# Attention stages of a decoder trunk: TensorE runs a unit's projection steps ahead of its scores

## Chip, cores and metric

The kernel runs on one core of a Trainium2 chip. The metric is the device time of one execution in microseconds (us). Every kernel was run several times; a time below is a median.

## What is computed

Two post-norm layers over 512 tokens of width 1024 in float32. Layer 0 mixes tokens with native sparse attention (16 heads of 64; a compressed branch, a selected branch and a window branch; for 512 tokens the last two see every earlier token). Layer 1 mixes with "forgetting" attention (a softmax with a cumulative gate bias). Each mixer is followed by a gated MLP with a causal convolution of width 3. Cut to what matters:

```
for i in range(2):
    y = nsa_mixer(x, ...) if i % 2 == 0 else fox_mixer(x, ...)
    x = layer_norm(ALPHA * x + y, ln1_g[i], ln1_b[i])
    x = layer_norm(ALPHA * x + conv_ffn(x, ...), ln2_g[i], ln2_b[i])

# nsa, per head:  q,k rotated;  softmax(q k / 8, causal) v  for ks,vs and for kw,vw,
#                 plus softmax(q k_cmp) v_cmp over 31 compressed blocks, three learned gates
# fox, per head:  softmax(q k / 8 + cum_q - cum_k, causal) v
```

## The kernel before

Every engine has its own instruction list, written out by hand, and the lists meet only at named semaphores. Activations lie transposed (width on the 128 partitions, 512 tokens along the row). A float32 operand is split into a high and a low part of type float32r, and each product is three matmuls: high x high, low x high, high x low (`mm3`, lines 908 to 911).

**A unit** is one attention block: a head's 128 queries against their keys, for one branch. In layer 0 (128 units) a head has eight: four query blocks i = 0 to 3, each for the selected and for the window branch; w = 0 to 7 is the unit's place in its head and i = w // 2. In layer 1 (64 units) a pair of heads has eight, v = 0 to 7, with i = v % 4. A unit goes through TensorE three times, with other engines in between:

- S, the scores (`nsa_scores`, `fox_scores`; lines 1067 and 1281, the bias 1282, the causal mask 1052);
- VectorE takes the row maximum (line 1425), ScalarE the exponential (line 625), VectorE the reciprocal of the sum (1433) and the scaling (1436 in layer 0, 1439 in layer 1);
- T, the transpositions of the probabilities (`turn`, line 1098, i + 1 of them);
- ScalarE copies the high part (line 640), VectorE takes the low part (`unit_lo`, line 1451, semaphore `pt_lo`);
- P, the value products (`pv`, 3(i + 1) small matmuls on lines 909 to 911; in every second unit of layer 0 a compressed product on line 1120 goes ahead of them).

In the loop step of unit u, TensorE runs S of u+2, then K, then P of u-2, then T of u. K is one of the projection steps (`kstep`, line 937) of later heads: three matmuls of 512 columns. Layer 0 has one K in each of the first 96 units, eight to a projected item. Layer 1 has four in v = 0 to 3 and two in v = 4 to 7 of pairs 0 to 6 (pair 0 lacks those of v = 0 and 1). At w = 0 and v = 0 T stands ahead of K.

The other engines keep the same beat: in the step of u, VectorE does max of u+2, scale of u+1 and low part of u-1; ScalarE does exp of u+2 and high part of u. Extra work is put at fixed places: in layer 0 ScalarE copies a finished item at w = 7, between exp of u+2 and the high part (`item_copy`, lines 595 and 597); VectorE computes the compressed branch's softmax from w = 4 on (`cmp_difference`, line 1473, at w = 5). In layer 1 ScalarE copies the projected values at v = 7 after exp of u+2 (`fox_value_copy`, line 847), and VectorE takes their low part at v = 1 after its max and scale (`fox_lo`, line 1714).

Three waits guard the projections' PSUM banks. K of w = 0 waits for the copy of the item before (`proj_copied`). The first K at v = 0 waits for the value copy (`proj_copied`), and the first K at v = 2 for the values' low part (`proj_lo`). GpSimd takes the low part of each weight block (line 433) once ScalarE has taken the high part (line 526), in layer 0 at w = 4.

Of the kernel before, what the change touches and what calls it, by code (L numbers as in the profile page):

```python
# [34 lines left out]
GROUPS, REP = 4, 4  # L35
# [15 lines left out]
R = 3  # L51
# [27 lines left out]
def build_trunk(nc, t, out):  # L79
    with ExitStack() as ctx:  # L80
# [3 lines left out]
        def sem(name):  # L84
            return ctx.enter_context(nc.semaphore(name))
# [130 lines left out]
        s_pf = sem("proj_copied")  # L216
# [690 lines left out]
        def _(pe):  # L907
            def mm3(o, ah, al, bh, bl, start, stop):
                nc.tensor.matmul(o, ah, bh, start=start, stop=False)  # L909
                nc.tensor.matmul(o, ah, bl, start=False, stop=False)  # L910
                return nc.tensor.matmul(o, al, bh, start=False, stop=stop)  # L911
# [25 lines left out]
            def kstep(c, slot, k, bank=BP):  # L937
                if k == 0:
                    pe.wait_ge(s_wl, c + 1)
                last = mm3(ps[:, bank, :], wh[:, slot, k, :], wl[:, slot, k, :], xh[:, k, :], xl[:, k, :], k == 0, k == KB - 1)  # L940
                if k == KB - 1:
                    last.then_inc(s_wu, 1)
# [108 lines left out]
            def mask(bank, i, stop=True):  # L1051
                return nc.tensor.matmul(ps[:, bank, i * P:(i + 1) * P], identb[:, :], causalb[:, :], start=False, stop=stop)  # L1052

            def nsa_scores(u):
                g, v = u // 32, u % 32
                h, i, br = v // 8, v % 8 // 2, v % 2
                par = g % 2
                if v % 8 == 0:

                    pe.wait_ge(s_pl, 4 * g + 3 + h // 2)  # L1060
                    if h == 0:
                        pe.wait_ge(s_sw[par], 32 * (g // 2 + 1))
                if u >= 2:
                    pe.wait_ge(s_ex, u - 1)
                n, b = (i + 1) * P, BS + u % 2
                for part in range(2):
                    nc.tensor.matmul(ps[:, b, 0:n], qs[par][:, h, i * P:n], (ks, kw)[br][par][:, part, 0:n], start=part == 0, stop=False)  # L1067
                mask(b, i).then_inc(s_sc, 1)

            def cmp_scores(H):  # L1070
                g, h = H // 4, H % 4
                rows = slice(h % 2 * HD, h % 2 * HD + HD)

                n = min(H + 3, NSA_ITEMS) - 1
                if n % 4 == 1:
                    pe.wait_ge(s_pl, n + 1)
                else:
                    pe.wait_ge(s_r2, n - (n + 2) // 4 + 1)

                pe.wait_ge(s_pf, 4 * g + 3 + h // 2)  # L1080
                for i in range(QT):
                    last = nc.tensor.matmul(ps[:, BX, i * NCMP:(i + 1) * NCMP], qf[g % 2][rows, h // 2, i * P:(i + 1) * P],
                                            kcd[rows, g * NCMP:(g + 1) * NCMP], start=True, stop=True)
                last.then_inc(s_cs, 1)

            def cmp_turn(H):

                pe.wait_ge(s_cp, H + 1)
                for i in range(QT):
                    last = nc.tensor.transpose(ps[0:NCMP, BX, i * P:(i + 1) * P], csm[:, i, :], ident[:, :])  # L1090
                last.then_inc(s_ct, 1)

            def turn(u, loc):
                pe.wait_ge(s_pr, u + 1)
                if not isinstance(u, int) or u >= 2:
                    pe.wait_ge(s_ptl, u - 1)
                for kt in range(loc[1] + 1):
                    last = nc.tensor.transpose(ps[:, BT + loc[0] % 2, kt * P:(kt + 1) * P], prob[:, loc[0] % 4, kt * P:(kt + 1) * P], ident[:, :])  # L1098
                last.then_inc(s_pt, 1)
# [10 lines left out]
            def nsa_pv(u):  # L1110
                g, v = u // 32, u % 32
                h, i, br = v // 8, v % 8 // 2, v % 2
                H = 4 * g + h
                bank = BO + H % 2
                if v % 8 == 0:
                    if H >= 2:
                        pe.wait_ge(s_ol, H - 1)
                    pe.wait_ge(s_cc, H + 1)
                if br == 0:
                    nc.tensor.matmul(ps[0:HD, bank, i * P:(i + 1) * P], vcd[:, g, :], pct[0:NCMP, H % 2, i * P:(i + 1) * P], start=True, stop=False)  # L1120
                cs = slice(br * HD, (br + 1) * HD)
                pv(u, (u, i), bank, vh[g % 2][:, :, cs], vl[g % 2][:, :, cs], False, br == 1)
# [10 lines left out]
            for g in range(GROUPS):  # L1133
                for v in range(32):
                    u = 32 * g + v
                    if u + 2 < NSA_UNITS:
                        nsa_scores(u + 2)
                    if v % 8 == 0:

                        turn(u, (u, v % 8 // 2))  # L1140
                    if g < GROUPS - 1:
                        n = 4 * (g + 1) + v // 8
                        if v % 8 == 0:
                            pe.wait_ge(s_pf, n)
                        kstep(4 + n, (4 + n) % R, v % 8)
                    if v % 8 == 4 and u + 4 < NSA_UNITS:
                        cmp_scores(u // 8 + 1)
                    if u >= 2:
                        nsa_pv(u - 2)
                    if v % 8 == 0:  # L1150
                        cmp_turn(u // 8)
                    else:
                        turn(u, (u, v % 8 // 2))
                    if v % 8 == 1 and (g < GROUPS - 1 or v == 1):

                        pe.wait_ge(s_cc, u // 8 + 1)
                        item_turn(*((g + 1, v // 8 - 1) if v > 1 else (g, 3)))
# [112 lines left out]
            def fox_scores(u, v, par, pair, rows_landed):  # L1270

                h, i = v // 4, v % 4
                if v == 0:
                    pe.wait_ge(s_pl, NSA_ITEMS + 3 * pair + 2)
                    pe.wait_ge(s_bl[par], rows_landed)
                if v == 4:
                    pe.wait_ge(s_plb, pair + 1)
                pe.wait_ge(s_ex, u - 1)
                n, b = (i + 1) * P, BS + v % 2
                for part in range(2):  # L1280
                    nc.tensor.matmul(ps[:, b, 0:n], fqs[par][:, h, i * P:n], fkd[par][:, h, part, 0:n], start=part == 0, stop=False)  # L1281
                nc.tensor.matmul(ps[:, b, 0:n], biasq[par][0:4, h, i * P:n], biask[par][0:4, h, 0:n], start=False, stop=False)  # L1282
                mask(b, i).then_inc(s_sc, 1)
# [11 lines left out]
            def fox_stages(pair, par, rows_next, first=False, more=True):  # L1295
                U = NSA_UNITS + 8 * pair
                for v in range(8):
                    if v + 2 < 8:
                        fox_scores(U + v + 2, v + 2, par, pair, None)
                    elif more:  # L1300
                        fox_scores(U + v + 2, v - 6, 1 - par, pair + 1, rows_next)
                    if v == 0:
                        turn(U + v, (v, v % 4))
                    if more:

                        for s in range(*FOX_STEPS[v]):
                            if first and s < KB:
                                continue
                            r, k = s // KB, s % KB
                            if k == 0 and r:  # L1310

                                pe.wait_ge(s_pl, NSA_ITEMS + 3 * (pair + 1) + r - 1)
                            if k == 0 and not r:

                                pe.wait_ge(s_pf, NSA_ITEMS + pair + 1)
                            kstep(C_FOX + 3 * (pair + 1) + r, (C_FOX + r) % R, k, (BP, BX, BP)[r])
                    if v >= 2:
                        fox_pv(U + v - 2, v - 2, par, pair)
                    elif not first:
                        fox_pv(U + v - 2, v + 6, 1 - par, pair - 1)  # L1320
                    if v:
                        turn(U + v, (v, v % 4))
                    if v == 0 and not first:

                        pe.wait_ge(s_plb, pair + 1)
                        value_turn(NSA_ITEMS + pair + 1)
# [9 lines left out]
            with pe.Fori(0, 3) as i:  # L1336
                for r in range(2):

                    fox_stages(1 + r + 2 * i, (1 + r) % 2, 32 * (2 + i))
# [489 lines left out]
```

## Time and profile before

| | |
|---|---|
| median of 3 runs | 1564.2 us (1561.87 to 1565.9) |
| span of the profiled execution | 1563.1 us |
| TensorE busy in it | 1489.1 us (95%) |
| VectorE, ScalarE, GpSimd busy | 860.3, 700.9, 598.0 us |
| layer 0, units with K | about 93 to 353 us of the span |
| layer 1, pairs 1 to 6 | about 917 to 1097 us, 30 us a pair |

The profile comes from one execution, so sums are made on its span of 1563.1 us; the median of the runs lies 1.1 us above it. A busy TensorE is not TensorE at its peak, since matmuls overlap: time is read from start to start. Line numbers are those of the kernel.

### The profile page before, as it was taken

Reading aid. Unit: us, or ns where it says so; the run is one execution under the profiler, and the core shown is the slowest. Engines: PE = TensorE matmul, PEld = TensorE weight load, DVE = VectorE, ACT = ScalarE, POOL = GpSimd, SP = SyncE. Lnnn points to the kernel's source line nnn. Section 1 sums busy time; section 2 is a strip of 40 time slices with the busy share of each in tenths; the row PEclk is TensorE's granted clock in tenths of the full one; section 3 lists DMA queues with packets and bytes.
Section 4 is the critical chain, followed back from the end, with each engine's and each line's share of the span. In section 5 each row is a group of like instructions: output and inputs, shape, how many; then the busy total and the mean of one; then the engine's idle time right before and its main releaser. Section 6 shows DMA issues by size and latency. Waiting matters only on the chain.

```text
span 1563.1 us, 22861 instructions
## 1 busy us (share of the span) xinstructions
PE 1489.1 (95%) x8010; PEld 1171.6 (75%) x8010; DVE 860.3 (55%) x1549; ACT 700.9 (45%) x1292; POOL 598.0 (38%) x294
## 2 busy tenths in 40 slices
PE   8989999998998999999998999999989999999997
PEld 6867676777756888888885677777757888888884
DVE  3268877787786434342136667777886433431134
ACT  3445555558434444443133555555334444442132
POOL 2442323220245444444446422222255444444441
PEclk9999999999999999999999899999999999999999
DMA  9321111100121333333332112111221333333321
GB/s 268 76 57 42 23 33 29 41 28 2 50 73 41 108 94 94 95 94 105 102 89 70 45 46 65 54 41 55 67 68 54 94 105 94 96 94 98 97 75 54
DMA packets 219065, 113.80 MB, mean 73 GB/s; under 512 B 23136, under 2 KB 216596, under 8 KB 218996
## 3 DMA queue, kind: packets, MB, share of 16 engines
q1 hardware_dynamic: 218356, 110.80, 24.9%
q10 hardware_dynamic: 640, 2.10, 0.5%
q8 instruction: 42, 0.69, 0.2%
q14 instruction: 27, 0.22, 0.0%
HBM read 108.55 MB, written 2.23 MB: 71 GB/s over the span
## 4 chain that ended last, share of the span: by engine, by line
PE 80%; DVE 12%; issue 3%; ACT 3%; POOL 1%; DMA 1%; SPq 0%; DVEq 0%; POOLq 0%; ACTq 0%
PE ps L909 22%; PE ps L911 21%; PE ps L910 21%; PE ps L1098 3%; PE ps L1067 2%; DVE cstat L1473 2%; PE ps L1282 1%; DVE z L1630 1%; PE ps L1281 1%; DVE negmax L1425 1%; DVE z L1608 1%; PE ps L1052 1%; PE ps L1162 1%; DVE z L1621 1%; PE ps L990 1%
## 5 line engine op out<-in xcount | busy, mean ns | idle before, releaser
L433 POOL TENSOR_TENSOR wl<-raw,wh 128x1024 fp32r<-128x1024 f32 (+1 forms) x196 | 468.5, 2391 | 782.2 <-ACT wh L526 782.0
L909 PE MATMUL ps<-xh,wh 128*128 128x512 f32 x1008 | 408.6, 405 | 2.0 <-POOL wl L433 2.0
L911 PE MATMUL ps<-xh,wl 128*128 128x512 f32 x1008 | 394.7, 392 | 0.0
L910 PE MATMUL ps<-xl,wh 128*128 128x512 f32 x1008 | 394.1, 391 | 0.0
L526 ACT ACTIVATE wh<-raw 128x1024 fp32r<-128x1024 f32 (+1 forms) x196 | 202.7, 1034 | 230.2 <-PE ps L911 212.1
L911 PEld LDWEIGHTS ps<-xh,wl 128*128 128x128 f32 x1008 | 190.0, 189 | 40.4
L909 PEld LDWEIGHTS ps<-xh,wh 128*128 128x128 f32 x1008 | 191.8, 190 | 37.7 <-issue 1.8
L910 PEld LDWEIGHTS ps<-xl,wh 128*128 128x128 f32 x1008 | 190.7, 189 | 34.3 <-issue 0.2
L1653 DVE SCALAR_TENSOR_TENSOR work<-ps,conv,work 128x511 f32<-128x511 f32 x88 | 66.0, 750 | 221.6 <-ACT work L772 157.6
L1425 DVE TENSOR_REDUCE negmax<-ps 128x1 f32<-128x128 f32 (+1 forms) x192 | 93.6, 488 | 108.4 <-PE ps L1052 105.9
L625 ACT ACTIVATE prob<-ps,negmax 128x128 f32<-128x128 f32 (+1 forms) x192 | 101.2, 527 | 102.4 <-DVE negmax L1425 100.5
L909 PE MATMUL ps<-gh,wh 128*128 128x512 f32 x352 | 138.6, 394 | 0.0
L911 PE MATMUL ps<-gh,wl 128*128 128x512 f32 x352 | 137.0, 389 | 0.0
L910 PE MATMUL ps<-gl,wh 128*128 128x512 f32 x352 | 137.0, 389 | 0.0
L640 ACT ACTIVATE pth<-ps 128x128 fp32r<-128x128 f32 (+1 forms) x192 | 83.5, 435 | 113.5 <-PE ps L1098 84.9
L1451 DVE TENSOR_TENSOR ptl<-ps,pth 128x128 fp32r<-128x128 f32 (+1 forms) x192 | 92.8, 483 | 3.7 <-ACT pth L640 3.0
L1098 PE MATMUL ps<-ident,prob 128*128 128x128 f32 x480 | 90.2, 287 | 2.5 <-DVE ptl L1451 1.7
L909 PE MATMUL ps<-pth,vh 128*64 128x128 f32 x320 | 68.4, 238 | 23.7 <-DVE ptl L1451 23.6
L775 ACT ACTIVATE gh<-work 128x512 f32 (+1 forms) x44 | 27.8, 632 | 119.0 <-DVE work L1665 119.0
L1678 DVE SCALAR_TENSOR_TENSOR z<-z,ps 128x512 f32<-128x512 f32 x10 | 6.9, 688 | 129.5 <-PE ps L911 129.5
L909 PEld LDWEIGHTS ps<-gh,wh 128*128 128x128 f32 x352 | 66.1, 188 | 14.6 <-issue 1.0
L910 PEld LDWEIGHTS ps<-gl,wh 128*128 128x128 f32 x352 | 66.1, 188 | 14.6 <-issue 1.0
(211 smaller groups left out, 2519.9 us busy)
## 6 DMA issues: line engine op xcount, KB each, us to landing
raw<-in_ffn_w_up SPq DMA_DIRECT2D x88, 512.0 KB, 3.8
raw<-in_ffn_w_down SPq DMA_DIRECT2D x32, 512.0 KB, 4.1
raw<-in_fox_w_in SPq DMA_DIRECT2D x24, 512.0 KB, 3.8
raw<-in_nsa_w_in SPq DMA_DIRECT2D x12, 512.0 KB, 5.0
raw<-in_ffn_w_down SPq DMA_DIRECT2D x16, 384.0 KB, 3.5
raw<-in_nsa_w_in SPq DMA_DIRECT2D x16, 256.0 KB, 3.7
raw<-in_nsa_w_o SPq DMA_DIRECT2D x8, 512.0 KB, 4.0
raw<-in_fox_w_o SPq DMA_DIRECT2D x8, 512.0 KB, 4.2
```

Of the source, the lines that this page charges most:

```text
L433: nc.gpsimd.tensor_tensor(wl[:, slot, 0:nk, :], raw[:, slot, 0:nk, :], wh[:, slot, 0:nk, :].bitcast(F32), ALU.subtract).then_inc(s_wl, 1)
L526: nc.scalar.activation(wh[:, slot, 0:nk, :], raw[:, slot, 0:nk, :], ACT.Copy).then_inc(s_wh, 1)
L625: nc.scalar.activation(prob[:, loc[0] % 4, 0:n], ps[:, BS + loc[0] % 2, 0:n], ACT.Exp, bias=negmax[:, loc[0] % 4:loc[0] % 4 + 1], accum_ou ...
L640: nc.scalar.activation(pth[:, loc[0] % 2, 0:n], ps[:, BT + loc[0] % 2, 0:n], ACT.Copy).then_inc(s_pth, 1)
L909: nc.tensor.matmul(o, ah, bh, start=start, stop=False)
L910: nc.tensor.matmul(o, ah, bl, start=False, stop=False)
L911: return nc.tensor.matmul(o, al, bh, start=False, stop=stop)
L1067: nc.tensor.matmul(ps[:, b, 0:n], qs[par][:, h, i * P:n], (ks, kw)[br][par][:, part, 0:n], start=part == 0, stop=False)
L1098: last = nc.tensor.transpose(ps[:, BT + loc[0] % 2, kt * P:(kt + 1) * P], prob[:, loc[0] % 4, kt * P:(kt + 1) * P], ident[:, :])
L1425: nc.vector.tensor_reduce(negmax[:, loc[0] % 4:loc[0] % 4 + 1], ps[:, BS + loc[0] % 2, 0:n], AX.X, ALU.max, negate=True).then_inc(s_nm, 1)
L1451: nc.vector.tensor_tensor(ptl[:, b, 0:n], ps[:, BT + b, 0:n], pth[:, b, 0:n].bitcast(F32), ALU.subtract).then_inc(s_ptl, 1)
L1653: nc.vector.scalar_tensor_tensor(out=buf[:, 1:SEQ], in0=ps[:, bank, 0:SEQ - 1], scalar=conv[:, l, 1, bass.ds(blk, 1)], in1=buf[:, 1:SEQ], ...
```

## The change

In the loops of both layers the K steps of a unit are moved to the front of the unit, ahead of S (and, at w = 0 and v = 0, ahead of T). The waits that K carries move with it. Nothing is added or removed, and no other engine's list is touched.

```
             for g in range(GROUPS):
                 for v in range(32):
                     u = 32 * g + v
-                    if u + 2 < NSA_UNITS:
-                        nsa_scores(u + 2)
-                    if v % 8 == 0:
-
-                        turn(u, (u, v % 8 // 2))
                     if g < GROUPS - 1:
                         n = 4 * (g + 1) + v // 8
                         if v % 8 == 0:
                             pe.wait_ge(s_pf, n)
                         kstep(4 + n, (4 + n) % R, v % 8)
+                    if u + 2 < NSA_UNITS:
+                        nsa_scores(u + 2)
+                    if v % 8 == 0:
+
+                        turn(u, (u, v % 8 // 2))
...
             def fox_stages(pair, par, rows_next, first=False, more=True):
                 U = NSA_UNITS + 8 * pair
                 for v in range(8):
+                    if more:
+
+                        for s in range(*FOX_STEPS[v]):
...
+                            if k == 0 and r:
+
+                                pe.wait_ge(s_pl, NSA_ITEMS + 3 * (pair + 1) + r - 1)
+                            if k == 0 and not r:
+
+                                pe.wait_ge(s_pf, NSA_ITEMS + pair + 1)
+                            kstep(C_FOX + 3 * (pair + 1) + r, (C_FOX + r) % R, k, (BP, BX, BP)[r])
                     if v + 2 < 8:
                         fox_scores(U + v + 2, v + 2, par, pair, None)
```

TensorE's list at the turn from w = 7 to w = 0 in layer 0. `ident,prob` is T, `ks,qs` is S, `xh,wh` begins K. Before:

```order
L1098 MATMUL ps<-ident,prob 128x128 x3
L1067 MATMUL ps<-ks,qs 128x256 [waits exps]
L1067 MATMUL ps<-ks,qs 128x256
L1052 MATMUL ps<-causalb,identb 128x128
L1098 MATMUL ps<-ident,prob 128x128 [waits pt_lo,probs]
L909 MATMUL ps<-xh,wh 128x512 [waits w_lo,proj_copied]
L910 MATMUL ps<-xl,wh 128x512
L911 MATMUL ps<-xh,wl 128x512
```

And now:

```order
L1098 MATMUL ps<-ident,prob 128x128 x3
L909 MATMUL ps<-xh,wh 128x512 [waits w_lo,proj_copied]
L910 MATMUL ps<-xl,wh 128x512
L911 MATMUL ps<-xh,wl 128x512
L1067 MATMUL ps<-ks,qs 128x256 [waits exps]
L1067 MATMUL ps<-ks,qs 128x256
L1052 MATMUL ps<-causalb,identb 128x128
L1098 MATMUL ps<-ident,prob 128x128 [waits pt_lo,probs]
```

K and its wait for the copied item now follow the last T of w = 7 directly.

TensorE's list in layer 1 from v = 7 to v = 0 (`fkd,fqs` and `biask,biasq` are S). Before:

```order
L1098 MATMUL ps<-ident,prob 128x128 x3
L1278 ISA
L1281 MATMUL ps<-fkd,fqs 128x384 [waits exps]
L1281 MATMUL ps<-fkd,fqs 128x384
L1282 MATMUL ps<-biask,biasq 128x384
L1052 MATMUL ps<-causalb,identb 128x128
L1096 REGISTER_ALU [waits probs]
L1098 MATMUL ps<-ident,prob 128x128 [waits pt_lo]
L1315 REGISTER_ALU
L939 ISA [waits proj_copied]
L909 MATMUL ps<-xh,wh 128x512 [waits w_lo]
```

And now:

```order
L1098 MATMUL ps<-ident,prob 128x128 x3
L1309 REGISTER_ALU
L939 ISA [waits proj_copied]
L909 MATMUL ps<-xh,wh 128x512 [waits w_lo]
L910 MATMUL ps<-xl,wh 128x512
```

S of v = 2 and T of v = 0 no longer stand between the last T of v = 7 and the wait for the value copy.

TensorE's list in layer 1 from v = 1 to v = 2. Before:

```order
L1098 MATMUL ps<-ident,prob 128x128
L1278 REGISTER_ALU [waits odd_keys_lo]
L1281 MATMUL ps<-fkd,fqs 128x128 [waits exps]
L1281 MATMUL ps<-fkd,fqs 128x128
L1282 MATMUL ps<-biask,biasq 128x128
L1052 MATMUL ps<-causalb,identb 128x128
L1312 REGISTER_ALU
L939 REGISTER_ALU [waits proj_lo]
L909 MATMUL ps<-xh,wh 128x512 [waits w_lo]
```

And now:

```order
L1098 MATMUL ps<-ident,prob 128x128
L1306 REGISTER_ALU
L939 REGISTER_ALU [waits proj_lo]
L909 MATMUL ps<-xh,wh 128x512 [waits w_lo]
L910 MATMUL ps<-xl,wh 128x512
```

The wait for the values' low part now stands ahead of S of v = 4 instead of behind it.

## Rows read from the trace of the kernel before

**Rows 1.** The profile page: its span.

```profile
span 1563.1 us, 22861 instructions
```

**Rows 2.** The list of waits, TensorE: total us, times, longest.

```profile
PE ps L909 <- DVE ptl L1451: 25.8, 23, 1.7
...
PE ps L1067 <- ACT prob L625: 2.5, 1, 2.5
```

**Rows 3.** Busy time by stretch: stretch, length, engines busy, clock, DMA; layer 1.

```profile
977.00:1007.00 30.00, 30.00 (x191) 23.61 (x190) 21.57 (x41) 16.73 (x38) 7.19 (x3) 1.00 0.19 53
```

**Rows 4.** Timeline, TensorE, layer 0, w = 6, 7: start, duration, instruction, wait.

```profile
190.41 0.42 PE L1067 MATMUL ps<-ks,qs 128*128 128x128 f32 x2
...
190.70 0.48 PE L909 MATMUL ps<-xh,wh 128*128 128x512 f32 x1
...
193.68 0.28 PE L909 MATMUL ps<-pth,vh 128*64 128x128 f32 x1 [1.67 <-DVE ptl L1451]
...
195.35 0.63 PE L910 MATMUL ps<-xl,wh 128*128 128x512 f32 x1
```

**Rows 5.** Timeline, VectorE, layer 0, the step of w = 5.

```profile
190.04 0.55 DVE L1436 TENSOR_SCALAR prob<-prob,rinv,gate 128x512 f32<-128x512 f32 x1
190.50 2.33 DVE L1473 TENSOR_SCALAR cstat<-cstat 128x4 f32<-128x4 f32 x1
```

**Rows 6.** The instructions of line 1473: count, shortest, median, longest in ns.

```profile
L1473 DVE TENSOR_SCALAR cstat<-cstat x16: 161/2331/2334, 84.6 to 387.8; 128x4 f32<-128x4 f32 x16
```

**Rows 7.** Timeline, GpSimd: one weight block in layer 0, one in layer 1.

```profile
190.29 2.51 POOL L433 TENSOR_TENSOR wl<-raw,wh 128x1024 fp32r<-128x1024 f32 x1 [0.87 <-ACT wh L526]
...
1008.99 2.40 POOL L433 TENSOR_TENSOR wl<-raw,wh 128x1024 fp32r<-128x1024 f32 x1 [6.55 <-ACT wh L526]
```

**Rows 8.** Timeline, TensorE: S behind K; P behind the mask.

```profile
89.42 0.33 PE L1067 MATMUL ps<-ks,qs 128*128 128x128 f32 x2
...
89.63 0.41 PE L1067 MATMUL ps<-kw,qs 128*128 128x128 f32 x2
...
379.95 0.25 PE L909 MATMUL ps<-pth,vh 128*64 128x128 f32 x1
380.04 0.23 PE L910 MATMUL ps<-ptl,vh 128*64 128x128 f32 x1
```

**Rows 9.** Timeline, TensorE, layer 0, w = 7: K, P, T, then S of the next unit.

```profile
173.98 0.47 PE L909 MATMUL ps<-xh,wh 128*128 128x512 f32 x1
...
174.76 0.23 PE L909 MATMUL ps<-pth,vh 128*64 128x128 f32 x1
...
175.30 0.62 PE L1098 MATMUL ps<-ident,prob 128*128 128x128 f32 x4
175.68 0.48 PE L1067 MATMUL ps<-ks,qs 128*128 128x256 f32 x2
```

**Rows 10.** Timeline, ScalarE, layer 0, w = 7: exp, then the item's copy.

```profile
174.59 0.37 ACT L625 ACTIVATE prob<-ps,negmax 128x128 f32<-128x128 f32 x1
...
174.96 0.60 ACT L597 ACTIVATE qf<-ps 128x512 f32<-128x512 f32 x1
```

**Rows 11.** Timeline, TensorE, layer 1, v = 1: the mask that ends S.

```profile
1008.08 0.23 PE L1052 MATMUL ps<-causalb,identb 128*128 128x128 bf16 x1
```

**Rows 12.** Timeline, ScalarE, layer 1, v = 7: exp, then the value copy.

```profile
1001.72 0.47 ACT L625 ACTIVATE prob<-ps,negmax 128x256 f32<-128x256 f32 x1 [0.90 <-DVE negmax L1425]
...
1002.19 0.59 ACT L847 ACTIVATE work<-ps 128x512 f32<-128x512 f32 x1
```

**Rows 13.** Timeline, VectorE, layer 1: max of v = 7; then the step of v = 1.

```profile
1001.28 0.41 DVE L1425 TENSOR_REDUCE negmax<-ps 128x1 f32<-128x256 f32 x1
...
1008.35 0.69 DVE L1425 TENSOR_REDUCE negmax<-ps 128x1 f32<-128x512 f32 x1 [3.54 <-PE ps L1052]
...
1009.14 2.46 DVE L1439 TENSOR_SCALAR prob<-prob,rinv 128x384 f32<-128x384 f32 x1
1011.52 0.68 DVE L1714 TENSOR_TENSOR fvl<-ps,fvh 128x512 fp32r<-128x512 f32 x1
```

More of the change, by code:

```diff
@@ L1297, in fox_stages @@
                 for v in range(8):
[L1298 to L1303, printed above, removed]
                     if more:
@@ L1316, in fox_stages @@
                             kstep(C_FOX + 3 * (pair + 1) + r, (C_FOX + r) % R, k, (BP, BX, BP)[r])
+                    if v + 2 < 8:
+                        fox_scores(U + v + 2, v + 2, par, pair, None)
+                    elif more:
+                        fox_scores(U + v + 2, v - 6, 1 - par, pair + 1, rows_next)
+                    if v == 0:
+                        turn(U + v, (v, v % 4))
                     if v >= 2:
```

## The prediction

> **What bounds the kernel now.** I read the list of waits first, then the stretches, then the timelines of one head and one pair. The span is 1563.1 us [rows 1] and TensorE is the engine that everything ends on. In the loops that the change touches it hardly waits. In layer 1 it is busy for all 30.00 us of a pair [rows 3]: the pairs last as long as TensorE's list. In layer 0 the list of waits holds 23 waits for `pt_lo`, 25.8 us in all [rows 2]; 12 of them are one and the same, 1.67 us ahead of P at w = 6 of each of the 12 heads with K [rows 4]. Behind it stands VectorE's line 1473, a four-column instruction that takes 2.33 us there and 0.161 us at its shortest [rows 5, 6]. It starts at 190.50, while GpSimd's weight block runs from 190.29 to 192.80, and it ends at 192.83 [rows 5, 7]. So a VectorE instruction of this kind that starts inside GpSimd's is held to its end.
>
> So TensorE has nothing to gain from doing the same work in another order, except at that wait and in the gaps between instructions. What must be asked is whether the other engines still deliver in time. Before, K stood between S and P: while K ran, the others had time for max, exp and scale of the scores just made. Now K stands between T and S. All that hangs on S starts one K later (0.78 us from 173.98 to 174.76 [rows 9], two to four times nearly as much in layer 1), and it still has to be done by the same P, T and K.
>
> **Gaps between instructions.** S behind K takes 0.21 us to the next S (89.42 to 89.63 [rows 8]); S behind T takes 0.29 us to K (190.41 to 190.70 [rows 4]), for the same 128 columns. That gives 0.08 us a unit. P behind the mask starts its second matmul after 0.09 us [rows 8], where nine matmuls of a P behind K take 0.54 us, 0.06 each (174.76 to 175.30 [rows 9]); that takes 0.03 back. K follows T instead of the mask; I cost that at nothing. So -0.05 us in each of 96 units of layer 0 and 54 of layer 1: **-7.5 us**. Each side rests on one or two rows; the ends are 0 and -12 (150 x 0.08).
> The Trainium skill (TensorE: Matmul & The Clock Gate, Back-to-back issue gap) has the gap follow from the columns of a matmul and its weight load, with nothing for a change of kind. By it this term would be zero and the sum 28 instead of 21. The two S above differ at equal columns, so I go by the rows.
>
> **The first unit.** At the first unit of layer 0 TensorE waits 2.5 us at S for an exponential [rows 2]; one K now runs inside that wait: **-0.8 us**.
>
> **P at w = 6, layer 0.** In the step of w = 5 VectorE does max of w = 7 (it waits for S), scale, line 1473, one more, the low part that P waits for. Scale starts now at 190.04, just ahead of GpSimd's start at 190.29 [rows 5, 7]. With S a K later, scale would start at about 190.75, inside GpSimd's instruction, whose own start hangs on T and ScalarE and does not move. A scale that starts inside one is held too: in layer 1 one started at 1009.14, just after GpSimd's 1008.99, and ended at 1011.60, 0.2 us after GpSimd's end at 1011.39 [rows 7, 13]. So scale ends near 193.0, line 1473 follows with 0.2 us, and from its end to P are 0.85 us (192.83 to 193.68 [rows 4, 5]): P at 194.05 instead of 193.68. Twelve heads at 0.37: **+4.5 us**. Bounds: 0 if scale still slips in, 0.7 (a whole K) if nothing of the delay is absorbed, 0 to +8.4.
>
> **K at w = 0, layer 0: a new wait.** K waits for the item copy, which ScalarE does at w = 7 behind exp of u+2, which waits for max, which waits for S; S now stands behind K at w = 7. From the mask of that S to the start of max are 0.27 us (1008.08 to 1008.35 [rows 11, 13]), from max to exp of 128 columns about 0.32 (an estimate: 0.44 for 256 columns, 1001.28 to 1001.72 [rows 12, 13], less 0.12 for half the columns), from exp to the copy 0.37 (174.59 to 174.96), the copy 0.60 [rows 10], and 0.05 to TensorE: 1.61. TensorE needs from that mask to the end of T 0.04 + 0.57 for P (0.54 + 0.03) + 0.38 for T (175.30 to 175.68 [rows 9]): 0.99. The wait is 0.62, before it was none, since S and T lay between. It comes in 11 heads (the first item is copied before the loop): **+6.8 us**. Bounds 0.3 and 0.9 a head, +3.3 to +10.
>
> **First K at v = 0, layer 1: a new wait.** The same with 256 columns: 0.27, 0.44, 0.47 to the copy (1001.72 to 1002.19), 0.59 for it [rows 12], 0.05: 1.82 after the mask. TensorE needs 0.04 + 0.39 for six matmuls of P + 0.38 for T: 0.81. The wait is at least 1.0. Max cannot start at once, though: in the kernel before it already started the moment VectorE was free, at 1001.28 [rows 13], and now VectorE's own work ahead of it, low parts that hang on S and K of v = 5 and 6, comes some 0.6 later while the mask falls at about 1001.1 (counted through from v = 4 in the same way). I take 1.4 us; six pairs (1 to 6): **+8.4 us**, bounds 0.8 and 1.7, +5 to +10.
>
> **First K at v = 2, layer 1: a new wait.** It waits for the values' low part, which VectorE does after max and scale of the step. From the mask: 0.27 to max, 0.79 to scale (1008.35 to 1009.14), 0.4 for an unheld scale (0.46 for 512 columns, 190.04 to 190.50 [rows 5]), 0.65 for the low part (0.68 [rows 13]), 0.05: 2.15. TensorE needs 0.04 + 0.75 for twelve matmuls + 0.17 for T: 0.96. Wait 1.15, six pairs: **+6.9 us**, bounds 0.9 and 1.4, +5.4 to +8.4. Before, four K lay behind the mask and covered it.
>
> **Small waits.** By the same counting P at w = 3, v = 5 and v = 7 find their low part within 0.2 us of the moment that they want it. I put 0.1 a head and 0.2 a pair, **+2.4 us**, 0 to 5. All other waits (S for its bank, T for the scaled probabilities, K at v = 4) keep over 1 us in this counting. S a K later loosens its own wait, which costs nothing now.
>
> **Sum.** -7.5 - 0.8 + 4.5 + 6.8 + 8.4 + 6.9 + 2.4 = +20.7 us on 1563.1, and with the 1.1 us between span and median 1564.2 + 20.7 = 1584.9, so **1585 us**, 1.3% slower. The term ends, added, give +1 to +41; they will not all fall to one side.
>
> **Rivals.**
>
> Faster: the new waits stay hidden. The point is whether the item and value copies end before the last T (0.99 and 0.81 us after the mask). That needs ScalarE and VectorE to be 0.6 to 1.4 us quicker than the rows, for instance if max could start on a part of S. Then the gaps and the first unit are left: -8.3, 1556 us. Against it: five links, each with its row, and in order on each engine.
>
> No change: the wait at w = 6 breaks up. If GpSimd's weight block started 1.3 us later in relation to VectorE (its ScalarE half slipping behind), scale and line 1473 would run ahead of it, and some 1.4 of the 1.67 us would go: 12 x 1.4 = 16.8, and the +4.5 with it, 20.7 - 21.3, about 1564 us. Against it: ScalarE takes that half from T of w = 4, ahead of the exp that comes late.
>
> Slower still: the clock. After the wait at 193.68 the second matmul of a K takes 0.63 us, longer than the 0.48 of the slower first one at 190.70 [rows 4]: the lower of the two levels, 1.2 GHz. Of the 12 equal waits in layer 0 two were followed by such a stretch; my estimate is 1.5 us lost in each (some 3 us of work at half speed). In layer 1, with no waits, the granted clock is 1.00 [rows 3]. Now layer 1 has 12 waits of over 1 us and layer 0 11 more. At two in twelve that is three or four more stretches, +5; at every second one +18: 1590 to 1603 us.
> [...]
>
> Partly: one of the four larger terms is absent: 1570 to 1578 us.
>
> That the change does nothing is excluded by TensorE's list.
>
> **Chances.** Forecast as worked out (1577 to 1591) 0.62; clock beyond that 0.12; partly 0.10; no change 0.08; faster 0.08. A measurement of this kernel can tell about 0.3% from no change, 4.7 us. Slower takes the first three less 0.01, 0.83; same 0.09; faster 0.08. The range takes in the forecast, most of partly and the first part of the clock case: 1569 to 1597.
>
> **What the profile will show.** The list of waits should name for line 909 ScalarE's copies (lines 595/597: 11 waits of 0.6; line 847: 6 of 1.4) and VectorE's line 1714 (6 of 1.1), and the waits for `pt_lo` at w = 6 should be near 2.1 us, with line 1436 or 1439 held by GpSimd instead of line 1473. A pair of layer 1 should last 32.3 instead of 30.0 us. I am wrong if these waits are absent, if the pairs keep 30 us, or if half-clock stretches outweigh the waits.

## The result

| | median of the runs | |
|---|---|---|
| before | 1564.6 us (1561.9 to 1565.9, 4 runs) | |
| after | 1594.0 us (1591.5 to 1599.1, 4 runs) | ratio 1.0199, 95% interval 1.0179 to 1.022 |

The changed kernel is 29.4 us slower: 1.9% by the medians, 2.0% by the ratio in the table. The forecast was 1585 us with a range of 1569 to 1597: the direction and the new waits were right, and the centre was 9 us low. The profiled execution of after took 1599.1 us with a span of 1597.3, 5 us above its median, so sums from traces are made on the spans: 1563.1 to 1597.3, +34.2 us. What sets this execution apart from the other three is the clock (see the sum below).

The page of after and its list of waits, TensorE (total us, times, longest), beside [rows 1, 2]:

```profile
span 1597.3 us, 22861 instructions
```

```profile
PE ps L909 <- DVE ptl L1451: 29.7, 30, 2.0
...
PE ps L909 <- ACT work L847: 6.4, 6, 1.1
PE ps L909 <- DVE fvl L1714: 6.1, 6, 1.0
...
PE ps L1067 <- ACT prob L625: 1.4, 1, 1.4
PE ps L909 <- ACT work L595: 1.3, 4, 0.4
...
PE ps L909 <- ACT qf L597: 0.7, 2, 0.4
```

Three entries are new, the three guards of the projections' banks: ScalarE's item copies (595, 597), its value copy (847), VectorE's low part of the values (1714). The first entry grew and the first unit's wait (1067) shrank. A recorded wait ahead of K begins at the modelled end of T, 0.24 us after the moment at which K could have started by start-to-start times: 1.06 recorded is 1.30 of delay.

**Layer 0, w = 6.** Timelines of VectorE, GpSimd and TensorE in after (start, duration, instruction, wait); they answer to [rows 4, 5, 7]:

```profile
173.18 2.37 POOL L433 TENSOR_TENSOR wl<-raw,wh 128x1024 fp32r<-128x1024 f32 x1 [0.19 <-ACT wh L526]
...
173.62 2.21 DVE L1436 TENSOR_SCALAR prob<-prob,rinv,gate 128x512 f32<-128x512 f32 x1
174.18 0.33 PE L1067 MATMUL ps<-ks,qs 128*128 128x128 f32 x2
174.36 0.23 PE L1052 MATMUL ps<-causalb,identb 128*128 128x128 bf16 x1
...
175.75 0.16 DVE L1473 TENSOR_SCALAR cstat<-cstat 128x4 f32<-128x4 f32 x1
...
176.14 0.55 DVE L1451 TENSOR_TENSOR ptl<-ps,pth 128x384 fp32r<-128x384 f32 x1
...
176.75 0.27 PE L909 MATMUL ps<-pth,vh 128*64 128x128 f32 x1 [1.80 <-DVE ptl L1451]
```

GpSimd's weight block starts at 173.18. The scaling, due just ahead of it before, starts 0.44 us behind its start and is held to its end (2.21 us where [rows 5] has 0.55). Line 1473 behind it takes 0.16 us instead of 2.33. So the hold changed its victim, and P waits 1.77 to 2.04 us instead of 1.67.

**A pair of layer 1.** Busy time by stretch, after: one whole pair from first K to first K (columns as in [rows 3]), and its three waits from the timeline of TensorE:

```profile
1062.16:1094.84 32.68, 30.36 (x188) 23.73 (x189) 16.97 (x41) 16.01 (x38) 7.15 (x3) 1.00 0.17 49
```

```profile
1062.16 0.49 PE L909 MATMUL ps<-xh,wh 128*128 128x512 f32 x1 [1.06 <-ACT work L847]
...
1072.92 0.49 PE L909 MATMUL ps<-xh,wh 128*128 128x512 f32 x1 [1.02 <-DVE fvl L1714]
...
1092.74 0.27 PE L909 MATMUL ps<-pth,fvh 128*64 128x128 f32 x1 [0.23 <-DVE ptl L1451]
```

A pair took 30.0 us without a pause in TensorE's busy time; now it takes 32.68 with 30.36 busy. The third wait, ahead of P at v = 7, is new as well.

**The clock.** Three stretches in layer 0 and two pairs in layer 1 show what the rest of the loss is made of; first after around the wait at 176.75, then a whole pair with a half-clock stretch and one without, in the kernel of experiment 2, which has the same layer 1:

```profile
174.00:177.00 3.00, 1.20 (x11) 0.84 (x10) 2.93 (x7) 0.78 (x4) 1.55 (x1) 1.00 0.07 14
177.00:180.00 3.00, 3.00 (x25) 2.72 (x23) 1.74 (x7) 1.23 (x5) 0.00 (x0) 0.66 0.76 161
180.00:183.00 3.00, 3.00 (x21) 2.53 (x20) 2.86 (x7) 1.54 (x5) 1.28 (x1) 0.77 0.00 0
```

```profile
978.32:1012.58 34.26, 31.94 (x189) 24.85 (x189) 16.97 (x41) 16.00 (x38) 7.14 (x3) 0.95 0.17 46
912.96:945.64 32.68, 30.36 (x188) 23.71 (x189) 16.97 (x41) 16.00 (x38) 7.14 (x3) 1.00 0.18 50
```

Behind the wait the granted clock falls to the lower level, 1.2 GHz, for some 3 us: 3 x 0.34 + 3 x 0.23 = 1.7 us of clock. The pair in which this happens takes 34.26 instead of 32.68, 1.58 us more. I added up 3 us x (1 - clock) over all stretches of 3 us with a clock below 0.97, up to the end of each trace's span: 21.8 us in before, 33.8 in after. In the heads with K and pairs 1 to 6 there are 2 such stretches before and 12 after (8 and 4).

**The sum on the spans.** A head of layer 0 without such a stretch takes mostly 20.96 us before and 21.64 after (20.54 and 21.36 where the item is values): 0.71 a head on the mean of eleven, +7.8. Six pairs at 2.68: +16.1. First unit: -1.1. Clock: +12.0. Together +34.8, measured +34.2.

The agreement is closer than the parts are. From its first T to that of the first unit without K, layer 0 takes 14.0 us more, where its waits (6.7) and six more half-clock stretches (10.2) add up to 16.9: in five heads such a stretch lies where the wait ahead of K at w = 0 would be, and no wait is recorded there. Pairs 0 to 6 of layer 1 take 22.1 us more. The rest of the span is 1.9 us shorter: before happens to have three stretches more there.

The clock also explains why the profiled execution of after is the slowest. Its mean granted clock is 0.979, that of the other three 0.982 to 0.983: they lose 27 to 29 us by (1 - clock) x span, some 5 to 7 us less than the profiled one. By this estimate the median has 22.8 us of waits and gaps and some 7 of clock, against 29.4 measured.

### The profile page after: what moved, and what is told of

The parts are those of the page before. It is cut to its first block, busy times and chain, and to the rows that moved or that the text cites. A ratio compares the mean times of both kernels' runs of the same rounds, so it can differ in the third digit from the quotient of the medians.

```text
span 1597.3 us, 22861 instructions
## 1 busy us (share of the span) xinstructions
PE 1503.6 (94%) x8010; PEld 1191.7 (75%) x8010; DVE 835.9 (52%) x1549; ACT 693.2 (43%) x1292; POOL 595.0 (37%) x294
## 4 chain that ended last, share of the span: by engine, by line
PE 78%; DVE 13%; issue 3%; ACT 3%; POOL 1%; DMA 0%; DVEq 0%; SPq 0%; ACTq 0%; POOLq 0%
PE ps L909 22%; PE ps L910 21%; PE ps L911 21%; PE ps L1098 2%; PE ps L1067 2%; DVE negmax L1425 2%; DVE prob L1436 2%; DVE z L1630 1%; PE ps L1282 1%; PE ps L1281 1%; DVE z L1608 1%; PE ps L1052 1%; PE ps L1162 1%; DVE ptl L1451 1%; PE ps L1120 1%
## 5 line engine op out<-in xcount | busy, mean ns | idle before, releaser
L909 PE MATMUL ps<-xh,wh 128*128 128x512 f32 x1008 | 416.2, 413 | 16.7 <-ACT work L847 6.4
L910 PE MATMUL ps<-xl,wh 128*128 128x512 f32 x1008 | 398.1, 395 | 0.0
L909 PEld LDWEIGHTS ps<-xh,wh 128*128 128x128 f32 x1008 | 192.9, 191 | 59.7 <-issue 19.2
L911 PEld LDWEIGHTS ps<-gh,wl 128*128 128x128 f32 x352 | 66.1, 188 | 13.7
```

## Experiments

The runs of the kernel before are those made beside each set. "S first" at some w or v means that there the scores stand ahead of K, as in the kernel before. w and v name the loop step; the S in it belongs to the unit two steps later. Diffs are against the changed kernel unless said.

### 1 and 2. One layer at a time

In experiment 1 the block of `fox_stages` is put back as it was (first diff) and layer 0 stays changed; in experiment 2 the loop of layer 0 is put back (second diff) and layer 1 stays changed.

```
                 for v in range(8):
+                    if v + 2 < 8:
+                        fox_scores(U + v + 2, v + 2, par, pair, None)
...
                     if more:
```

```
                     u = 32 * g + v
+                    if u + 2 < NSA_UNITS:
+                        nsa_scores(u + 2)
...
                     if g < GROUPS - 1:
```

> K ahead of S in layer 0 only; layer 1 in the order of before. Theory W (the cost is waits: K waits for the item copy at w = 0, P at w = 6 waits longer behind a scale that GpSimd holds, and half-clock stretches come after waits): the distance from one wait at w = 6 to the next, in heads without a half-clock stretch, stays at 21.6 us instead of 21.0, six or so stretches more in this layer; 1574 to 1580 us. Rival G (the cost lies in TensorE's own list: more time between matmuls in the new order and a clock that falls with that order, not with waits): the 96 units of this layer get their share by number of K steps, 96 of 248, which is 11 of the 29 us, 1576 us; the time alone does not tell the two apart here, the place of the loss does.

> K ahead of S in layer 1 only; layer 0 in the order of before. Theory W: six waits of about 1.0 us idle for the value copy, six for the values' low part, a pair without a half-clock stretch lasts 32.7 us instead of 30.0, and up to four stretches of 1.6 us: 16 to 23 us, 1581 to 1588 us. Together with the run of layer 0 alone the two losses add up to that of the whole change, within 3 us. Rival G: 18 us here, 1583 us; again told apart by the place of the loss only.

Measured: layer 0 alone 1573.3 us (1572.8 to 1574.7), ratio 1.0055 [1.0036, 1.0074]; layer 1 alone 1587.8 us (1584.0 to 1588.4), ratio 1.0141 [1.0117, 1.0164]. The differences, 9.0 and 23.5 us, add up to 32.5, where the whole change has 29.4. The waits are those of after, each in its own layer, which is the place that theory W named. Layer 0 alone has seven half-clock stretches in its heads, layer 1 alone four in its pairs. By the sum above, layer 1 alone is 16.1 for the pairs and 29.1 - 21.8 = 7.3 of clock, 23.4; its span is 23.3 longer. Layer 0 alone is 7.8 - 1.1 and 5.7 of clock, 12.4, where its span is 9.8 longer: there part of the half-clock time lies under waits that would have been there anyway.

### 3. S first again where the guards are fed

Further down the same calls are made for the other units only (not shown).

```
+                    early = u + 2 < NSA_UNITS and v % 8 in (7,)
+                    if early:
+                        nsa_scores(u + 2)
...
                 for v in range(8):
+                    if v in (1, 7):
+                        if v + 2 < 8:
+                            fox_scores(U + v + 2, v + 2, par, pair, None)
```

> As the change, but in the units just ahead of a guarded K (w = 7 in layer 0, v = 7 and v = 1 in layer 1) S stands ahead of K again, as before; K itself stays first everywhere else, also at w = 0, v = 0 and v = 2 where it carries its wait. Theory W: S of the unit ahead now starts a K earlier, so the copies and the low part are ready when K wants them: no waits for them, few half-clock stretches in layer 1; what stays is 0.1 to 0.4 us a head at w = 6: 1561 to 1569 us. Rival G: 200 of 248 K steps are still in the new order, so most of the loss stays: 1583 us or more.

Measured: 1579.1 us (1578.3 to 1586.5), ratio 1.0107 [1.0075, 1.0139]. A miss for theory W's price, and below rival G's 1583. With S first at w = 7, v = 1 and v = 7 the waits for the item copy and for the values' low part are gone from the list but for one of 0.2 us, as expected. The one ahead of the first K of v = 0 is not touched at all:

```profile
PE ps L909 <- DVE ptl L1463: 29.2, 30, 2.0
PE ps L909 <- ACT work L847: 6.4, 6, 1.1
```

(Line 1463 is line 1451 of the kernel before; the numbers move with the edit.) So the value copy is not late because the S at v = 7 is late, along which the forecast had counted the first 1.0 us of this wait.

### 4. S first at w = 5 and v = 5 too

```
-                    early = u + 2 < NSA_UNITS and v % 8 in (7,)
+                    early = u + 2 < NSA_UNITS and v % 8 in (5, 7)
...
-                    if v in (1, 7):
+                    if v in (1, 5, 7):
```

(The lines with a minus are those of experiment 3.)

> The run with the guards' units back left layer 1's wait for the value copy as it was (1.06 us, six times), against what theory W expected of it. New theory V: that wait does not hang on S at v = 7 but on S at v = 5. K ahead of it delays max and exp at v = 5, and in ScalarE's list the odd head's key copies (line 824) and a weight block (line 526), 2.2 us together, stand behind that exp and ahead of the exp of v = 6 and 7; VectorE's low part of the keys and its max of v = 7 follow. This run puts S first at w = 5 and 7 in layer 0 and at v = 1, 5 and 7 in layer 1, K first elsewhere. Theory V: no waits on line 847 or 1714, a pair lasts 30.0 us or a little under, P at w = 6 waits 1.67 us again: 1561 to 1567 us. Rival: the wait comes from K at v = 4 or 6 as much, so that it stays at 0.5 us or more: 1568 to 1576 us.

Measured: 1574.3 us (1572.7 to 1578.7), ratio 1.0064 [1.0043, 1.0085]. A miss as well, and what the rival said: the wait is 1.06 us in each of six pairs, a pair takes 31.4 to 31.5 us, and in layer 0 P at w = 6 still waits 1.74 to 1.94 us. The timeline of VectorE and TensorE in layer 1, from the mask of the S at v = 4 on, shows why an S at its old place does not help:

```profile
997.04 0.23 PE L1052 MATMUL ps<-causalb,identb 128*128 128x128 bf16 x1
997.31 0.56 DVE L1437 TENSOR_REDUCE negmax<-ps 128x1 f32<-128x384 f32 x1 [1.68 <-PE ps L1052]
...
998.24 1.38 DVE L1713 TENSOR_TENSOR fkd<-ps,fkd 64x512 fp32r<-64x512 f32 x2
998.76 0.23 PE L1052 MATMUL ps<-causalb,identb 128*128 128x128 bf16 x1
...
1000.25 0.68 DVE L1437 TENSOR_REDUCE negmax<-ps 128x1 f32<-128x512 f32 x1
```

The mask at v = 5 stands at 998.76, but its max starts at 1000.25: VectorE is still busy with what hung on the S at v = 4. One late S hands its lag to the next, whichever order that one has.

### 5. Where the lag of the value copy comes from

Two kernels with layer 0 as before and, in layer 1, K first at v = 0, 2, 3 and 6 in the one, and at v = 0, 2 and 3 in the other. The line by which they differ:

```
-                    if v in (1, 4, 5, 7):
+                    if v in (1, 4, 5, 6, 7):
```

> Layer 0 as before; in layer 1 the projection steps run first only at v = 0, 2, 3 and 6, and the scores first at v = 1, 4, 5 and 7. Theory (VectorE and ScalarE have no spare time between the scores of v = 4 and the value copy, so that one K ahead of any of these scores is handed on to the copy): with S first at v = 4 too, the 1.06 us ahead of the first K of v = 0 and the 1.02 us ahead of the first K of v = 2 are gone, a pair takes 30.0 us again (31.4 with S first at v = 1, 5 and 7), and the time is that of the kernel before, 1562 to 1566 us. Rival (K first at v = 6 alone is enough, its two matmul groups standing ahead of the scores of the next pair's first head): about 0.5 to 1.06 us of the wait stay in each of six pairs, a pair takes 30.5 to 31.4 us, 1567 to 1574 us.

> Layer 0 as before; in layer 1 the projection steps run first only at v = 0, 2 and 3, and the scores first at v = 1 and 4 to 7. In the trace of the kernel before, T at v = 7 starts at 1001.66, so K could start 0.38 us later, at 1002.04, while ScalarE's value copy (line 847) ends at 1002.78 and K, seen in the run with S first at v = 1, 4, 5 and 7, starts 0.14 us behind its end: 1002.92. Theory (K first at v = 0 uncovers 0.88 us of lag that was there all along, and K first at v = 6, two groups of it, adds the other 0.4 us by holding VectorE's and ScalarE's lists back): the wait ahead of the first K of v = 0 is recorded with 0.6 to 0.7 us instead of 1.06 (0.24 us of each such wait lie inside the modelled end of T), a pair takes 30.7 to 30.9 us instead of 31.34, and the time is 1568 to 1571 us. Rival (the wait hangs on v = 0 alone, or on something later than the scores): it stays at 1.06 us, a pair at 31.3 us, 1571 to 1574 us. Second rival (it hangs on v = 6 alone): no wait is left, a pair takes 30.0 us, 1563 to 1566 us.

Measured: with K first at v = 6 too, 1573.8 us (1569.8 to 1574.4), ratio 1.0049 [1.0032, 1.0066]; without it 1569.0 us (1564.9 to 1571.2, 10 runs), ratio 1.0027 [1.0013, 1.0042]. In the first the wait is 1.06 to 1.07 us in each pair and a pair takes 31.34 us (the rival held, the theory fell); in the second 0.64 us, as the theory for it said, and 30.55 us a pair, a little less than its 30.7. The timelines around v = 6, first kernel and second (here line 1433 is max, 1709 the keys' low part):

```profile
999.47 0.23 PE L1052 MATMUL ps<-causalb,identb 128*128 128x128 bf16 x1
...
999.74 0.29 DVE L1433 TENSOR_REDUCE negmax<-ps 128x1 f32<-128x128 f32 x1 [2.94 <-PE ps L1052]
...
1000.14 0.49 DVE L1447 TENSOR_SCALAR prob<-prob,rinv 128x512 f32<-128x512 f32 x1
...
1000.66 1.40 DVE L1709 TENSOR_TENSOR fkd<-ps,fkd 64x512 fp32r<-64x512 f32 x2
...
1003.03 0.41 DVE L1433 TENSOR_REDUCE negmax<-ps 128x1 f32<-128x256 f32 x1
...
1003.93 0.59 ACT L847 ACTIVATE work<-ps 128x512 f32<-128x512 f32 x1
...
1004.66 0.50 PE L909 MATMUL ps<-xh,wh 128*128 128x512 f32 x1 [1.07 <-ACT work L847]
```

```profile
999.38 0.23 PE L1052 MATMUL ps<-causalb,identb 128*128 128x128 bf16 x1
999.65 0.29 DVE L1433 TENSOR_REDUCE negmax<-ps 128x1 f32<-128x128 f32 x1 [1.56 <-PE ps L1052]
...
1001.18 1.40 DVE L1709 TENSOR_TENSOR fkd<-ps,fkd 64x512 fp32r<-64x512 f32 x2 [0.64 <-ACT fkd L824]
...
1004.46 0.59 ACT L847 ACTIVATE work<-ps 128x512 f32<-128x512 f32 x1
...
1005.19 0.49 PE L909 MATMUL ps<-xh,wh 128*128 128x512 f32 x1 [0.64 <-ACT work L847]
```

In the second the keys' low part waits for ScalarE (0.64 us of slack at that place). In the first VectorE idles 2.94 us for the mask, which stands behind two K, and then runs from there to the max of v = 7 with no gap: max, scaling, the keys' low part (1.40 us), the low part for P, the output's addition. So the wait ahead of the first K of v = 0 has two parts: 0.88 us (0.64 recorded) of lag that the kernel before had as well, under S and T at v = 0, which K first uncovers, and 0.42 us that K first at v = 6 adds through VectorE's list. The S at v = 7 has no part in it: in after, its mask is at 1059.60 and its max starts only at 1060.52. K first at v = 0 alone was not run; the first part rests on this kernel and on the trace of the kernel before, where T at v = 7 starts at 1001.66, K could have started 0.38 us later, at 1002.04, and the value copy ends at 1002.78 [rows 12]:

```profile
1001.66 0.62 PE L1098 MATMUL ps<-ident,prob 128*128 128x128 f32 x4
```

### 6. Taking the hold out of VectorE's way

GpSimd's weight block starts when ScalarE's high part is done, in layer 0 at w = 4. Three kernels move that high part in the kernel before to w = 5, 6 and 7; a fourth moves it to w = 5 in the changed kernel.

```
-                    if g < GROUPS - 1 and w == 4:
+                    if g < GROUPS - 1 and w == 7:
                         c = 4 + 4 * (g + 1) + v // 8
                         hi(c + 2
```

> The kernel before, with ScalarE's high part of a weight block in layer 0 moved from w = 4 to w = 5, so that GpSimd's low part of it starts a unit later. Theory W: line 1473 and the low part ahead of P at w = 6 run before GpSimd starts; the wait of 1.67 us there goes in 12 heads and is not given back, since P of the units behind has over 2 us to spare: 1543 to 1550 us. Rival (the wait is set by the transposition and ScalarE's copy, and GpSimd only happens to end with it): no change, 1564 us.

> The kernel before, with that high part moved to w = 6. With w = 5 the wait of 1.67 us at w = 6 was gone and 0.7 to 1.3 us came back at T of w = 0, since GpSimd then held line 1482 at w = 6. With w = 6 GpSimd starts late in w = 7 and holds VectorE at w = 0, where TensorE's step is the longest (3 us): the returned wait shrinks to under 0.5 us: 1543 to 1549 us. Rival: any hold of 2.4 us costs about 1 us somewhere: 1549 to 1555 us.

> The kernel before, with that high part moved to w = 7. GpSimd holds VectorE at w = 0 and 1, just ahead of the rotation's step at w = 2: a wait of 0.5 to 1 us comes back: 1548 to 1556 us. Rival: TensorE's long step at w = 0 covers it: 1543 to 1549 us.

> The whole change, with ScalarE's high part of a weight block in layer 0 moved from w = 4 to w = 5. Theory W with its clock part (half-clock stretches follow TensorE's waits): the wait of 1.8 to 2.0 us at w = 6 goes, most of it coming back at w = 0, where the hold now delays max and so the item copy; a head lasts 20.9 us instead of 21.6, with no stretch or two in layer 0 instead of eight, four in layer 1 as before: 1575 to 1585 us. Rival G (the clock falls with the order of the list): layer 0 keeps its eight stretches: 1585 us or more.

Measured: 1551.8 us (ratio 0.9913 [0.9891, 0.9935]) at w = 5, 1542.9 (0.9858 [0.9829, 0.9887]) at w = 6, 1538.0 (0.9829 [0.9801, 0.9856]) at w = 7. At w = 5 theory W was right that the wait goes and wrong that nothing comes back: T of w = 0 waits 0.71 to 1.27 us in the heads with K (0.58 in the last), and the time is 2 us above its range. At w = 6 the forecast held, and at w = 7 the time is better than both expectations written for it; at neither is a wait recorded in the heads with K. Most heads take 20.23, 19.54 and 19.22 us. The changed kernel with w = 5: 1579.7 us, ratio 1.0106 [1.0065, 1.0147], as expected. Its layer 0 has no half-clock stretch, in the same new order, so rival G falls. VectorE and GpSimd of the kernel with w = 7:

```profile
187.68 0.35 DVE L1436 TENSOR_SCALAR prob<-prob,rinv,gate 128x128 f32<-128x128 f32 x1
187.94 0.68 DVE L1451 TENSOR_TENSOR ptl<-ps,pth 128x512 fp32r<-128x512 f32 x1
188.53 2.39 POOL L433 TENSOR_TENSOR wl<-raw,wh 128x1024 fp32r<-128x1024 f32 x1 [7.42 <-ACT wh L526]
189.93 0.43 DVE L1425 TENSOR_REDUCE negmax<-ps 128x1 f32<-128x256 f32 x1 [1.30 <-PE ps L1052]
190.27 0.15 DVE L1433 RECIPROCAL rinv<-psumrow 128x1 f32<-128x1 f32 x1
190.46 0.60 DVE L1436 TENSOR_SCALAR prob<-prob,rinv,gate 128x256 f32<-128x256 f32 x1
```

The same 2.39 us now fall into a place where VectorE has nothing of this kind to do: its next scaling starts 0.46 us ahead of GpSimd's end and takes 0.60. The Trainium skill (SBUF — State Buffer, "SBUF: two separate sides") describes an exclusive lock between GpSimd and certain VectorE instructions, held for a whole instruction by the one that starts first; the held instructions of these traces (2.33, 2.21 and 2.15 us where the unheld take 0.16 to 0.55) agree with it. No half-clock stretch is left in the heads with K: 2 before, none with the high part at w = 7, and the clock's loss over the span falls from 21.8 to 13.8 us. In the changed kernel with w = 5 the lag moves on: the P wait goes and the item copies are waited for with 1.15 to 1.75 us.

### 7. The order alone, without that hold

Two kernels with the high part at w = 7: layer 0 in the changed order and layer 1 as before, and K first only where it seemed free (in layer 0 at w = 0 to 6, in layer 1 at v = 0, 2, 3 and 6). The mixed one, against experiment 3:

```
-                    if v in (1, 7):
+                    if v in (1, 4, 5, 7):
...
-                    if g < GROUPS - 1 and w == 4:
+                    if g < GROUPS - 1 and w == 7:
```

> Layer 0 in the changed order, layer 1 as before, and ScalarE's high part of the weight block (so GpSimd's low part behind it) at w = 7 instead of w = 4. Beside the kernel before with that one move (1538.0 us) this prices the order alone, with the wait for the low part of the probabilities at w = 6 gone. Theory (the wait of 0.6 us ahead of K at w = 0 is the order's own cost, and gaps of 0.05 us in 96 units and 0.8 us in the first unit are its own gain; the half-clock stretches came from the waits at w = 6): 11 x 0.6 - 4.8 - 0.8 = +1 us, 1536 to 1541 us, and no more half-clock stretches in layer 0 than the other kernel has. Rival (a late item copy also throws the clock, or the weight block at w = 7 stands behind that copy on ScalarE and comes late for the next K): 1545 to 1556 us.

> The weight block's high part at w = 7, and the new order only where it should leave no wait: in layer 0 K first at w = 0 to 6 and S first at w = 7, in layer 1 K first at v = 0, 2, 3 and 6. Theory: the gaps of 84 units of layer 0 give 4.2 us and the first unit 0.8, and no wait is added, so 1532 to 1535 us beside 1538.0 for the weight block's move alone. Rival (VectorE's list in layer 0 has no spare time from w = 4 on either, as in layer 1): waits of 0.3 to 0.6 us a head come back ahead of P or K, 1537 to 1545 us.

Measured: layer 0 in the changed order 1556.5 us (1555.7 to 1558.0), 18.5 above the 1538.0 of the high part at w = 7 alone; the mixed order 1551.4 us (1549.2 to 1553.6), 13.5 above it. Both theories missed, and so did both rivals. The first kernel has no half-clock stretch in the heads, so the 1.5 us by which a head is longer (20.7 against 19.2) are waits less the gaps:

```profile
174.12 2.37 POOL L433 TENSOR_TENSOR wl<-raw,wh 128x1024 fp32r<-128x1024 f32 x1 [7.12 <-ACT wh L526]
174.25 0.15 DVE L1433 RECIPROCAL rinv<-psumrow 128x1 f32<-128x1 f32 x1
...
174.44 2.15 DVE L1436 TENSOR_SCALAR prob<-prob,rinv,gate 128x128 f32<-128x128 f32 x1
...
176.50 0.68 DVE L1451 TENSOR_TENSOR ptl<-ps,pth 128x512 fp32r<-128x512 f32 x1
...
177.23 0.27 PE L909 MATMUL ps<-pth,vh 128*64 128x128 f32 x1 [0.60 <-DVE ptl L1451]
```

The scaling at w = 0, which ran ahead of GpSimd's block (187.68 against 188.53 in the fence above), comes a K later, starts 0.32 us behind it, and is held: P at w = 1 waits. Measured from T to T against the kernel with the old order, that step is 0.75 us longer, the step with K's wait for the item copy 0.62, and three steps in which P finds its low part only just done (w = 3, 5 and 6) are 0.09 to 0.14 longer; the other three timed steps are 0.05 to 0.08 us shorter. In the mixed kernel the same scaling starts 0.08 us ahead of GpSimd's block in every fourth head and is held all the same (2.54 us), at 0.98 us for P. Its heads cost 6.0 us in all, and its pairs, 31.33 us as in experiment 5, 8.1: together 14.1, less the first unit's gain.

## Why the prediction came out as it did

- **Two new waits: right.** K at w = 0 was worked out as 0.62 and is 0.60 us (0.36 recorded). Six of eleven heads show it in after; the other five have a half-clock stretch just ahead of it, in which ScalarE can catch up. The first K of v = 2 was 1.15 and is 1.26.
- **First K of v = 0: right in size, by luck.** 1.4 forecast, 1.30 measured, six times. At least 1.0 of it was counted along the S at v = 7, and the rest was put on VectorE's low parts that hang on v = 5 and 6. Experiments 3 and 4 put S at v = 7 and 5 back and changed nothing. What the second route adds is 0.42 us and comes in at v = 6, two K ahead of one S. The larger part, 0.88 us, had been there before, hidden by S and T at v = 0.
- **P at w = 6: right mechanism, too large.** The scaling is held instead of line 1473, as worked out, but the wait grows from 1.67 to 1.77 to 2.04 us, mostly 1.80: some 0.13 where the sum had 0.37.
- **Small waits: too small.** P waits for its low part in three steps of a head, 0.09 to 0.14 us each (experiment 7), where I put 0.1 a head. In a pair the step of v = 5 is 0.18 us longer and that of v = 7 0.40, from T to T, where I put 0.2 for both. In layer 0 the two errors cancel: 7.7 us forecast for the heads (4.5 + 6.8 + 1.2 - 4.8), 7.8 measured. In layer 1, 13.8 forecast (8.4 + 6.9 + 1.2 - 2.7), 16.1 measured.
- **The gaps: right.** S to mask behind K takes 0.18 us (174.18 to 174.36) instead of 0.25 (the 0.29 of [rows 4] less the 0.04 from the mask to K), and the steps of experiment 7 without a new wait are 0.05 to 0.08 us shorter. The rule of the Trainium skill (TensorE: Matmul & The Clock Gate, Back-to-back issue gap), which knows no such difference, would have made them equal.
- **The first unit:** -0.8 forecast, 2.5 to 1.4 measured, -1.1.
- **The clock: the step that failed.** The sum left it out and gave it 0.12 as a rival, at two stretches in twelve waits. Without the clock the sum should have been +22.8 on the spans, against +20.7; with it, +34.8 in the profiled execution. At the median the clock is some 7 us of the 9 us by which the forecast was low. In layer 1 four of five pairs that could be timed from wait to wait had a stretch of 1.58 us, in layer 0 eight of twelve heads. In the loops "every second one", the upper case of the rival, was the nearer: ten stretches more. The ratio of the old waits was carried over, although the new ones come more densely: two a pair instead of none, two a head instead of one.

The rivals "faster" and "no change" fell by the waits that the list shows, and "partly" because all four larger terms are there. What the experiments add is why the change gains nothing: 0.05 to 0.08 us a step is all that the order gives, and every partial order tried pays more than that in waits of engines that keep the same beat. That no order at all could keep the gaps and add no wait is not shown.

## What to carry to other kernels

When a step is moved ahead of what feeds the other engines, follow the lag through each engine's whole list and not only from the instruction just ahead of the wait: a late instruction two or three steps earlier can set it, and restoring the nearest step then changes nothing. Look at what stood ahead of a guarded instruction before: it hid lag that no list of waits shows. And where a short VectorE instruction takes 2.3 us, moving the GpSimd instruction that it meets can be worth more than the order of TensorE's list: here one number in the kernel gave 27.1 us (1565.1 to 1538.0, 1.7%), and none of the orders tried gave anything.

## What was not expected of the hardware

- Half-clock stretches come behind waits that are short and regular, and not behind all of them. Each count is that of one execution. Twelve waits of 1.67 us, one in 21 us: 2 to 4 stretches (before and the kernels of experiments 2 and 5). With 1.74 to 2.05 us: 4, 6, 7 and 8 (experiments 4, 3, 1, after). Two waits of 1.06 and 1.02 us in each pair of 32.7 us: 3, 4 and 4 in six pairs (experiment 6's changed kernel, 2, after). One of 1.06 us in some 31.4 us, or of 0.64 us in 30.55: none in layer 1's pairs (experiments 3, 4, 5, 7). But the changed kernel with the high part at w = 5 has waits of 1.15 to 1.75 us in layer 0 and no stretch there. What decides stays open. The Trainium skill (TensorE: Matmul & The Clock Gate, HAM oscillation) describes a loop that runs at the lower clock in each of its steps, behind waits longer than any named here; with the shorter waits of these pairs, half to two thirds of the pairs had a stretch.
- The hold between VectorE and GpSimd can also strike a VectorE instruction that by the profile starts just ahead of GpSimd's. First the mixed kernel of experiment 7, then the second kernel of experiment 5:

```profile
149.70 2.54 DVE L1448 TENSOR_SCALAR prob<-prob,rinv,gate 128x128 f32<-128x128 f32 x1
149.78 2.38 POOL L433 TENSOR_TENSOR wl<-raw,wh 128x1024 fp32r<-128x1024 f32 x1 [16.59 <-ACT wh L526]
```

```profile
950.97 0.42 DVE L1447 TENSOR_SCALAR prob<-prob,rinv 128x384 f32<-128x384 f32 x1
951.04 2.60 POOL L433 TENSOR_TENSOR wl<-raw,wh 128x1024 fp32r<-128x1024 f32 x1 [7.45 <-ACT wh L526]
```

The one that starts 0.08 us ahead is held, in three heads alike; the one that starts 0.07 us ahead runs at full speed, in all six pairs of experiment 5, and there GpSimd's takes 2.60 us instead of 2.38. So the two starts as recorded do not say which of them gets through when they are this near. With 0.25 us between them ([rows 5, 7]: 190.04 and 190.29, 0.55 us) VectorE's is free.
